# Second block of a two-model kernel: the last two units of the output projection and the first two units of the MLP computed by halves of the tokens, with the norm between them by halves too

## What is computed

```python
merged = jax.nn.sigmoid(g_attn) * y_attn + jax.nn.sigmoid(g_ssm) * y_ssm
x = x + rmsnorm_2(merged @ w_out[l], norm_mix_post[l])
h = rmsnorm_2(x, norm_mlp_pre[l])
f = jnp.square(jax.nn.relu(h @ w_ff_in[l])) @ w_ff_out[l]
x = x + rmsnorm_2(f, norm_mlp_post[l])
```

## Time and profile before

| | us |
|---|---|
| median of 3 runs (lowest, highest) | 2342.88 (2342.22, 2343.38) |
| profiled execution, its own time | 2340.86 |
| its span, first to last instruction | 2339.1 |
| PE busy | 2297.5 (98%) |
| DVE / ACT / POOL busy | 1256.0 / 839.3 / 859.8 |

### The profile page before, as it was taken

How to read it: one execution, slowest core, us unless ns; L and a number is a source line. 1 busy time by engine, 2 the same in 40 slices (tenths; PEclk the granted TensorE clock), 3 DMA queues, 4 the chain that set the end, 5 groups by cost and what they waited for, 6 DMA issues and landing times.

```text
span 2339.1 us, 28137 instructions
## 1 busy us (share of the span) xinstructions
PE 2297.5 (98%) x11073; PEld 1881.6 (80%) x11073; DVE 1256.0 (54%) x1571; ACT 839.3 (36%) x1014; POOL 859.8 (37%) x200
## 2 busy tenths in 40 slices
PE   7999999999999999999999999999999998999998
PEld 6889777888888888887768888887888777888887
DVE  6677445554436745774455643468555653630533
ACT  5333435332232242333353323222335644422332
POOL 1332223334444443221333444444442333443443
PEclk9999999999999999999999999999999999999999
DMA  6333133454445544331334444445783334444442
GB/s 149 84 68 66 37 73 72 91 107 91 97 100 113 153 104 90 73 69 40 72 70 87 96 96 101 90 111 144 159 168 73 72 73 90 90 90 90 101 106 72
DMA packets 193145, 218.05 MB, mean 93 GB/s; under 512 B 14608, under 2 KB 165272, under 8 KB 192408
## 3 DMA queue, kind: packets, MB, share of 16 engines
q1 hardware_dynamic: 192856, 216.63, 42.3%
q10 hardware_dynamic: 192, 0.05, 0.0%
HBM read 206.92 MB, written 9.73 MB: 93 GB/s over the span
## 4 chain that ended last, share of the span: by engine, by line
PE 49%; issue 34%; POOL 8%; DVE 4%; DMA 1%; SPq 1%; ACT 1%; DVEq 1%; POOLq 0%; ACTq 0%
PE psG L363 15%; PE psG L365 15%; PE psG L364 15%; POOL w_lo L2751 8%; PE psH L650 3%; DMA raw<-in_w_in_dram 1%; SPq L1950 1%; DVE tab L1687 0%; DVE sq L453 0%; PE psH L2142 0%; ACT w_hi L356 0%; PE psH L675 0%; PE psH L2106 0%; DVE s L1687 0%; DMA raw<-in_w_down_dram 0%
## 5 line engine op out<-in xcount | busy, mean ns | idle before, releaser
L2751 POOL TENSOR_TENSOR w_lo<-raw,w_hi 128x2048 fp32r<-128x2048 f32 x184 | 853.0, 4636 | 1459.9 <-ACT w_hi L356 1388.0
L363 PE MATMUL psG<-h_hi,w_hi 128*128 128x512 f32 x1648 | 652.6, 396 | 12.0 <-DVE h_lo L500 7.9
L356 ACT CAST w_hi<-raw 128x2048 fp32r<-128x2048 f32 x184 | 351.0, 1908 | 827.0 <-PE psG L365 797.3
L364 PE MATMUL psG<-h_lo,w_hi 128*128 128x512 f32 x1648 | 643.6, 391 | 0.0
L365 PE MATMUL psG<-h_hi,w_lo 128*128 128x512 f32 x1648 | 643.2, 390 | 0.0
L363 PEld LDWEIGHTS psG<-h_hi,w_hi 128*128 128x128 f32 x1648 | 310.4, 188 | 96.4 <-issue 28.7
L365 PEld LDWEIGHTS psG<-h_hi,w_lo 128*128 128x128 f32 x1648 | 310.3, 188 | 65.6
L364 PEld LDWEIGHTS psG<-h_lo,w_hi 128*128 128x128 f32 x1648 | 310.7, 189 | 64.2 <-issue 1.4
L2688 DVE TENSOR_TENSOR hq<-r 128x512 f32<-128x512 f32 x32 | 84.9, 2691 | 148.8 <-ACT r L2459 148.8
L363 PE MATMUL psG<-hid_hi,w_hi 128*128 128x512 f32 x352 | 138.0, 392 | 1.7 <-POOL w_lo L2751 1.7
L365 PE MATMUL psG<-hid_hi,w_lo 128*128 128x512 f32 x352 | 137.0, 389 | 0.0
(11 more groups left out here) (476 smaller groups left out, 3276.7 us busy)
## 6 DMA issues: line engine op xcount, KB each, us to landing
raw<-in_w_in_dram SPq DMA_DIRECT2D x121, 512.0 KB, 6.4
raw<-in_w_gate_dram SPq DMA_DIRECT2D x44, 512.0 KB, 5.9
raw<-in_w_up_dram SPq DMA_DIRECT2D x44, 512.0 KB, 6.5
raw<-in_w_down_dram SPq DMA_DIRECT2D x32, 512.0 KB, 6.2
raw<-in_w_ff_in_dram SPq DMA_DIRECT2D x32, 512.0 KB, 6.3
raw<-in_w_ff_out_dram SPq DMA_DIRECT2D x32, 512.0 KB, 5.9
raw<-in_w_o_dram SPq DMA_DIRECT2D x16, 512.0 KB, 5.7
raw<-in_w_down_dram SPq DMA_DIRECT2D x16, 384.0 KB, 5.3
```

The costliest lines, as they stand in the source:

```text
L356: act.copy(w_hi[:, s, :], raw[:, s, :]).then_inc(hi_done.sem, 1)
L363: pe.matmul(out, a_hi, b_hi, start=first, stop=False)
L364: pe.matmul(out, a_hi, b_lo, start=False, stop=False)
L2751: pool.tensor_tensor(w_lo[:, s, :], raw[:, s, :], w_hi[:, s, :].bitcast(F32), ALU.subtract)\
```

## The change

Tokens are split into a first half (0 to 255) and a second half (256 to 511). PE now makes units 2 and 3 of `w_out` for the first half of the tokens, then both for the second, and the same for MLP 0 and MLP 1. A unit's half has as many matmuls as a whole unit had, with 256 columns each. The norm's two sums and its spreading are done once for each half: the first half's beside the second half of units 2 and 3, the second half's inside the first half of MLP 0 (`column_sums(1)` ahead of its third row block, `spread_half(1)` ahead of its seventh). ACT and DVE do their work on those tiles in halves, 128 x 256 an instruction. The cast of MLP 1 moves from DVE to ACT. `spread` moves to memory of its own, since `h_hi`, where it lay, is now written while it is in use. The diff, without most of the lines that it takes out (the section above describes them):

```diff
-    spread = nc.alloc_sbuf_tensor_at("spread", [P, TB, P], F32, offset=h_hi_at)
+    spread = at("spread", 12, [P, TB, P])
...
-        for k in range(4):
+        for k in range(2):
             pe_feature(pe, *un(V_WO + k), *jn(K_WO + k), m2_hi, m2_lo, merged_tile if k == 0 else None,
                        by_tile=k == 0)
 
-        def column_sums(tile, first, last):
...
+        def out_half(u, half, tiles):
+            m, s = un(V_WO + u)
+            jm, b = jn(K_WO + u)
+            if half == 0:
+                unit_ready(pe, m, s)
+                bank_ready(pe, jm, b)
+            wh = w_hi[:, s, :].rearrange("p (k c) -> p k c", k=KD)
+            wl = w_lo[:, s, :].rearrange("p (k c) -> p k c", k=KD)
+            t = slice(HALF * half, HALF * half + HALF)
+            for j in tiles:
+                if half:
+                    pe.wait_ge(y_sq.sem, 2 * u + j + 1)
+                for k in range(KD):
+                    c = slice(j * P, (j + 1) * P)
+                    mm = triple(pe, psG[:, 2 * b + j, t], wh[:, k, c], wl[:, k, c], m2_hi[:, k, t], m2_lo[:, k, t],
+                                k == 0, k == KD - 1)
+                mm.then_inc((tick if half else y_half).sem, 1)
+
+        def column_sums(half):
+            pe.wait_ge(y_dve.sem, 2 * half + Y_SUM)
+            pe.wait_ge(y_sq.sem, 8 + 4 * half)
+            for tile in (0, 6, 7):
+                for c in (2 * half, 2 * half + 1):
+                    mm = pe.matmul(psH[:, c, 0:2], sq_y2[:, tile, c * P:(c + 1) * P], ones[:, 0:2],
+                                   start=tile == 0, stop=tile == 7)
+            mm.then_inc(y_pe.sem, 1)
+
+        def spread_half(half):
+            pe.wait_ge(y_act.sem, 2 * half + Y_DG)
+            pe.matmul(psH[:, 2 * half, 0:HALF], ones[:, 0:1].broadcast_to([P, P]),
+                      spread[:, 2 * half:2 * half + 2, :].rearrange("p t c -> p (t c)"), start=True, stop=True)\
+              .then_inc(y_pe.sem, 1)
+
+        def mlp_half(u, half):
+            m, s = un(V_FA + u)
+            jm, b = jn(K_FA + u)
+            if half == 0:
+                unit_ready(pe, m, s)
+                bank_ready(pe, jm, b)
+            wh = w_hi[:, s, :].rearrange("p (k c) -> p k c", k=KD)
+            wl = w_lo[:, s, :].rearrange("p (k c) -> p k c", k=KD)
+            t = slice(HALF * half, HALF * half + HALF)
+            for k in range(KD):
+                if half == 0 and u == 0 and k == 2:
+                    column_sums(1)
+                if half == 0 and u == 0 and k == 6:
+                    spread_half(1)
+                if u == 0:
+                    pe.wait_ge(n_lo.sem, n_lo.at(DEPTH, KD + KD * half + k + 1))
+                for j in range(2):
+                    c = slice(j * P, (j + 1) * P)
+                    mm = triple(pe, psG[:, 2 * b + j, t], wh[:, k, c], wl[:, k, c], h_hi[:, k, t], h_lo[:, k, t],
+                                k == 0, k == KD - 1)
+                    if half and k == KD - 1:
+                        mm.then_inc(tick.sem, 1)
+
+        out_half(2, 0, (0, 1))
+        out_half(3, 0, (0, 1))
+        out_half(2, 1, (0,))
+        column_sums(0)
+        out_half(2, 1, (1,))
+        spread_half(0)
+        out_half(3, 1, (0, 1))
+        for half in range(2):
+            for u in range(2):
+                mlp_half(u, half)
...
+        def out_read(n, t):
+            b, j = jn(K_WO + n // 2)[1], n % 2
+            act.activation(y2[:, n, t], psG[:, 2 * b + j, t], ACT.Copy, scale=par[:, R_POST2 + n:R_POST2 + n + 1])
+            act.activation(sq_y2[:, n, t], psG[:, 2 * b + j, t], ACT.Square).then_inc(y_sq.sem, 1)
+            if j and (n == 1 or n == 3 or t.start):
+                act.drain().then_inc(psum_free[b].sem, 1)
+
+        for n in range(4):
+            act.wait_ge(tick.sem, Tn(V_WO + n // 2, n % 2))
+            out_read(n, slice(0, S))
+            if n % 2:
+                act.drain().then_inc(y_ok.sem, 1)
+                split_next(act, V_WO + n // 2)
+        first, second = slice(0, HALF), slice(HALF, S)
+
+        def mean_root(half):
+            act.wait_ge(y_pe.sem, 2 * half + Y_SS)
+            act.activation(y_col[:, 0, 2 * half:2 * half + 2], psH[:, 2 * half:2 * half + 2, 0], ACT.Sqrt,
+                           scale=1.0 / D, bias=eps_ap).then_inc(y_act.sem, 1)
+
+        def diagonals(half):
+            act.wait_ge(y_dve.sem, 2 * half + Y_RS)
+            for c in (2 * half, 2 * half + 1):
+                mm = act.activation(spread[:, c, :], ident[:, :], ACT.Copy, scale=y_col[:, 1, c:c + 1])
+            mm.then_inc(y_act.sem, 1)
+
+        def mlp_hi(k, half):
+            t = (first, second)[half]
+            act.wait_ge(x2_ok.sem, KD * half + k + 1)
+            act.activation(h_hi[:, k, t], xT[:, k, t], ACT.Copy, scale=par[:, R_MPRE2 + k:R_MPRE2 + k + 1])\
+               .then_inc(n_hi.sem, 1)
+
+        for n in range(4, 8):
+            act.wait_ge(y_half.sem, n - 3)
+            out_read(n, first)
+        act.drain().then_inc(y_ok.sem, 1)
+        act.activation(small[:, 62:63], eps_ap, ACT.Sqrt)
+        act.wait_ge(tick.sem, Tn(V_WO + 2, 0))
+        out_read(4, second)
+        mean_root(0)
+        diagonals(0)
+        split_next(act, V_WO + 2)
+        out_read(5, second)
+        for k in range(3):
+            mlp_hi(k, 0)
+        act.wait_ge(tick.sem, Tn(V_WO + 3, 0))
+        out_read(6, second)
+        for k in range(3, 5):
+            mlp_hi(k, 0)
+        act.wait_ge(tick.sem, Tn(V_WO + 3, 1))
+        out_read(7, second)
+        act.drain().then_inc(y_ok.sem, 1)
+        split_next(act, V_WO + 3)
+        mlp_hi(5, 0)
+        mean_root(1)
+        mlp_hi(6, 0)
+        diagonals(1)
+        mlp_hi(7, 0)
         for k in range(KD):
-            act.wait_ge(x2_ok.sem, k + 1)
-            gained_hi(act, DEPTH, KD, k, xT, par[:, R_MPRE2:R_MPRE2 + KD])
+            mlp_hi(k, 1)
...
+        dve.wait_ge(y_sq.sem, 4)
+        tt(sq_y2[:, 0:2, :], sq_y2[:, 0:2, :], sq_y2[:, 2:4, :], ALU.add)
+        dve.drain()
+        tt(sq_y2[:, 0, :], sq_y2[:, 0, :], sq_y2[:, 1, :], ALU.add)
+        dve.drain()
+
+        def add(out, x, y):
+            return dve.scalar_tensor_tensor(out=out, in0=x, scalar=1.0, in1=y, op0=ALU.mult, op1=ALU.add)
+
+        def fold_half(half):
+            t = slice(HALF * half, HALF * half + HALF)
+            dve.wait_ge(y_sq.sem, 6 + 4 * half)
+            add(sq_y2[:, 4, t], sq_y2[:, 4, t], sq_y2[:, 5, t])
             dve.drain()
-        tt(sq_y2[:, 0, :], sq_y2[:, 0, :], sq_y2[:, 1, :], ALU.add).then_inc(y_dve.sem, 1)
-        m, s = un(V_FA)
-        dve.wait_ge(lo_done.sem, m * 2 + (s + 1 + lo_done.credit))
-        m, s = un(V_FA + 1)
-        dve.wait_ge(raw_in[s].sem, m * 32 + 32)
-        dve.wait_ge(tick.sem, Tn(V_WO + 3, 1))
-        dve.tensor_copy(w_hi[:, s, :], raw[:, s, :]).then_inc(hi_done.sem, 1)
-        dve.wait_ge(y_act.sem, Y_SD)
-        dve.reciprocal(y_col[:, 1, :], y_col[:, 0, :]).then_inc(y_dve.sem, 1)
-        dve.wait_ge(y_ok.sem, 4)
-        dve.wait_ge(y_pe.sem, Y_SP)
-        for k in range(KD + 1):
-            if k < KD:
-                tt(psH[:, 1 + k % 2, :], y2[:, k, :], psH[:, 0, :], ALU.mult)
-                dve.drain()
-                tt(xT[:, k, :], xT[:, k, :], psH[:, 1 + k % 2, :], ALU.add).then_inc(x2_ok.sem, 1)
-            if k:
-                gained_lo(dve, DEPTH, KD, k - 1, xT, par[:, R_MPRE2:R_MPRE2 + KD])
+            add(sq_y2[:, 0, t], sq_y2[:, 0, t], sq_y2[:, 4, t]).then_inc(y_dve.sem, 1)
+
+        def mean_inverse(half):
+            c = slice(2 * half, 2 * half + 2)
+            dve.wait_ge(y_act.sem, 2 * half + Y_SD)
+            dve.reciprocal(y_col[:, 1, c], y_col[:, 0, c]).then_inc(y_dve.sem, 1)
+
+        fold_half(0)
+        mean_inverse(0)
+        for half in range(2):
+            t = slice(HALF * half, HALF * half + HALF)
+            dve.wait_ge(y_ok.sem, 3 + half)
+            dve.wait_ge(y_pe.sem, 2 * half + Y_SP)
+            for k in range(KD + 1):
+                if k < KD:
+                    mid = psH[:, 1 + 2 * half, HALF * (k % 2):HALF * (k % 2) + HALF]
+                    tt(mid, y2[:, k, t], psH[:, 2 * half, 0:HALF], ALU.mult)
+                    dve.drain()
+                    tt(xT[:, k, t], xT[:, k, t], mid, ALU.add).then_inc(x2_ok.sem, 1)
+                if k:
+                    dve.wait_ge(n_hi.sem, n_hi.at(DEPTH, KD + KD * half + k))
+                    dve.scalar_tensor_tensor(out=h_lo[:, k - 1, t], in0=xT[:, k - 1, t],
+                                             scalar=par[:, R_MPRE2 + k - 1:R_MPRE2 + k],
+                                             in1=h_hi[:, k - 1, t].bitcast(F32), op0=ALU.mult, op1=ALU.subtract)\
+                       .then_inc(n_lo.sem, 1)
+                if half == 0 and k == 3:
+                    fold_half(1)
+                if half == 0 and k == 7:
+                    mean_inverse(1)
```

67 lines of the change are left out of this document (4 added, 63 removed).

## The result

The changed kernel takes 2349.17 us, the median of 13 runs (2346.69 to 2357.74). The kernel before took 2342.88 in its 13 runs beside them (2339.98 to 2348.53). The ratio is 1.0032, with a 95% interval of 1.0024 to 1.0039. By the ratio that is 7.5 us slower; the two medians are 6.3 apart. The forecast was 2350.5 and "slower". The profiled execution took 2351.19 us, its span 2349.4.

The account below looks back on a forecast made before the run. PE, busy 98% of the span, was taken as the bound. DVE's pass, 16.5 us longer and 7.1 earlier, less 2.2 of ACT's slack, put MLP 2 about 7.6 later: 2348.5 profiled, 2350.5 median; range 2345.8 to 2355.5.

Parts of the forecast that it names:

- Step 1: PE at unit 3: its low part comes at 1950.60 but is wanted at 1948.1, a wait of 2.6 us.
- Step 2: Units 2 and 3 by halves: DVE may start its first-half pass at 1963.9, 7.1 us earlier, the gain.
- the clock stays down: Rival: PE's close waits lower its clock, 1.5 to 3 us at the first, +10 to +14 in all; chance 0.11.
- Steps 3 and 5: DVE's first and sixth low parts, held until POOL's low parts of MLP 0 and 1 end: holds of 3.4 and 4.1 us.
- Step 4: Next tiles and fold: ACT reads unit 3's last half tile late, so PE's second column sums wait 3.4 us.
- That sign: In the profile after: PE waits of over 3 us for column sums and for `h_lo`, clock at 0.50 after.
- Step 6: Serial chain between halves: DVE's second pass starts 2.6 us after the first half's last `xT`, then takes 9.0 us.
- Prices: Assumed half-instruction costs: PE matmul 0.1165 us, DVE 0.42 and 1.22 a tile, ACT tile read twice 0.65, high part 0.42.
- The end: Squares end at 1999.8, MLP 2's cast starts at 2000.0, and PE starts MLP 2 7.6 us later than before.
- no hold: Rival: DVE's low parts are not held beside POOL; MLP 2 starts 0.6 us earlier, 2342.3 us; chance 0.12.
- One hold only: Rival: only one of DVE's two low parts is held by POOL; +2.8 to +3.5 us, near 2346; chance 0.07.
- real gain: Rival: over 0.2% (4.7 us) faster; without PE waits behind 1950.7, MLP 2 starts 4.9 us earlier; chance 0.02.

Follow-up runs that it names:

- POOL only writes for MLP 0: The changed kernel with POOL's low part of MLP 0 replaced by memsets, that of MLP 1 left as it is: 2346.90 us, ratio 1.0026.
- the execution without a hold: The changed kernel with POOL's low parts of MLP 0 and MLP 1 both replaced by memsets: 2342.98 us, ratio 1.0008.
- the tuned version: The changed kernel with each half's `xT` first, unit 2's second-half tile 0 ahead of unit 3, column sums and second root retimed: 2338.29 us, ratio 0.9982.

## Why the prediction was right

The forecast mechanism is what happened, and the sum was 1.3 us off the median. A part of that closeness is luck: the pass started 1.8 us later than reckoned, and smaller misses behind it took 1.4 of them back. Point by point:

- **Step 1**, the wait for unit 3's weights: 2.6 forecast, 2.30 measured.
- **Step 2**, DVE's pass earlier. Forecast 7.1 us, measured 5.3 (39.61 to 34.35). The step missed that the clock would fall in unit 3's first half. In three executions with the same order and the same 2.30 us wait it did not fall, and their pass starts after 32.88 to 32.91 us; where it fell, after 34.31 and 34.35. That is 1.4 of the 1.8 us. This mishap stood among the rivals, as the first stage of "the clock stays down", at 1.5 to 3 us; the forecast's own case did not have it.
- **Steps 3 and 5**, the holds: forecast 3.8 and 4.5 us for the two low parts, measured 3.66 and 4.47; behind POOL's end 0.3 forecast, 0.3 measured. On the whole pass the two cost 4.9 us, not 7.5 (below). The experiments show the cause from three sides: taken away by letting POOL only write, by moving other instructions beside POOL, and brought into the kernel before by one add. The Trainium skill, page "SBUF — State Buffer", section "Who interferes with whom", states that a VectorE instruction with two SBUF inputs contends with a GpSimd instruction that reads SBUF and not with one that only writes; these runs agree, with 3.66 and 4.47 us beside the low part and 0.48 beside the memset.
- **Step 4**, PE's wait for the squares: 3.4 forecast, 3.21 measured. The other long wait of PE in the forecast, 3.6 us for the sixth low part, did not come: it was 0.23, because PE's column sums and the row blocks behind them ran at half clock and filled the time. That sign failed; with the clock up, in "POOL only writes for MLP 0", PE does wait 3.22 us there.
- **Step 6**, from the first half's last `xT` to the second pass: 2.6 forecast, 2.06 measured (1987.65 to 1989.71). The whole pass: 31.5 forecast, 30.8 measured.
- **Prices.** DVE 0.42 us and a tile 1.23, as reckoned. On ACT half a tile read twice takes 0.75 us and a single high part 0.51, each 0.1 more than reckoned. A half matmul costs 0.120, the upper end of what was kept, not 0.1165. (Where the prediction counts PE's half tiles it says ten, and its own 288 matmuls are twelve; its sum does not use this.)
- **The end.** The squares end at 2003.19 (2000.9 on the clock before, 1999.8 forecast), the cast stands right behind them and waits for nothing of PE, and from it to MLP 2 it is 6.69 us (6.8 to 7.2 forecast). MLP 2 starts 8.07 us later, forecast 7.6.

Behind the right sum one thing was wrong, how much of the holds lies on the path. The *no hold* rival was priced at 0.6 us faster, and the run gives a path 1.7 us longer (69.72), and a time 1.9 us longer by a ratio whose interval still holds 1. Its pass was to last 24.0 us (31.5 less 3.4 and 4.1) and lasts 25.9. The prediction took both holds as lying on the path in full. In fact a second chain, column sums, root, diagonals and spreading with PE at half clock, ended 2.19 us behind DVE's own work in the execution without a hold, and 1.7 us of the second hold were hidden beside it. In the case with both holds the two views give the same time, so the sum could not show the error. *One hold only* was too cheap as well: +2.8 to +3.5 forecast, +6.4 measured. The 2.9 us above 3.5 are 2.3 from the base without a hold, 1.4 from the clock at unit 3 and 1.1 behind the pass, less 1.9 since the hold added 2.2 and not 4.1. The *real gain*, at most 4.9 us if everything else were free, was a bound for the changed kernel's order and no run tests it. But the idea was worth nearly as much: the tuned version has a path 3.9 us shorter by another order, and by PE adding some squares that DVE folded.

Its loss was thus not in the idea of halving the norm, but in the order of three queues. The change moved POOL's reading from ahead of DVE's pass into it, and put ACT's cast ahead of a high part for which DVE stood waiting.

What stays open: how much of the time without a hold is the clock's. The stretches at half clock differ from execution to execution (last column but one of the table), and no run here compares one order with and without them.
